# Two attentions: where the lower weight halves stand on DVE, when turned probabilities are copied, and how output pieces are laid between the turnings

## The chip, the cores and the metric

The kernel runs on one core of a Trainium2 chip. The metric is the device time of one execution in microseconds (us), lower is better. Five engines work from queues of their own and meet at semaphores: TensorE (PE, with PEld for its weight loads), DVE (vector), ACT (scalar), GpSimd (POOL) and SP, which only issues transfers here.

## What is computed

Two transformer blocks over 256 tokens of width 1024, in f32, batch 1. What matters here are the two attentions.

```python
# first block: neighbourhood attention (8 heads) beside a windowed one (8 heads, sinks)
proj = h @ w_in[l] + b_in[l]
qa, ka, va, qb, kb, vb, ga, gb = jnp.split(proj, IN_SPLITS, axis=-1)
y_na = neighbourhood_attention(qa, ka, va, na_rpb[l]) @ w_branch_na[l]
y_swa = windowed_gqa_with_sink(qb, kb, vb, swa_sink[l]) @ w_branch_swa[l]
mixed = jax.nn.sigmoid(ga) * y_na + jax.nn.sigmoid(gb) * y_swa
# second block, layer 1: causal window of 128 keys, 16 heads, sinks
q = rope((h @ w_q[j]).reshape(B, S, N_Q_HEADS, HEAD_DIM), cos, sin)
m = swa_sink_attention(q, kk, vv, sinks[j]) @ w_o[j]
```

## The kernel before

All weights are read once, as a stream of units of 128 x 2048 f32 (1 MB). SP loads a unit into one of three buffers `w32` (`load_unit`, L515 and after); ACT writes its upper half `w_hi` (`split`, L675: a copy rounded to the engine's reduced f32), DVE subtracts for its lower half `w_lo` (`split`, L1619). A product is then three matmuls: upper half by the lower part of x, upper by upper, lower by upper (`product`, L1030 to L1032, 256 columns; `wide_product`, L1042 to L1044, 512 columns). A buffer is loaded again once its lower half is made (`w_lo_ready`). `next_split(at, n)` splits the unit three ahead of n.

Every engine's order is written out by hand. Both attentions run in eight periods, p = 0 to 7, of two heads each:

- TensorE: scores of the next pair (`score1`, L1279; `score2`, L1544, with the mask added by a matmul, L1547), then the turning (transpose) of head 2p's probabilities and of head 2p+1's (`turn`, L1290), then both attends (`attend_pair`, L1302). Matmuls of other work stand between them. In the first attention that is one half of a gate unit (`gate_tile`, 24 matmuls) behind each turning. In the second it is the query units U_Q+2 and U_Q+3 (periods 0 and 1, with `partners`, L1507, for the rotation) and then 32 pieces of the output projection. A piece (`out_chunk(q, c, t)`, three wide matmuls) adds chunk c (heads 2c, 2c+1) to half q of the width, for token half t, and the table `out_behind` says which pieces stand ahead of the first turning, behind it, and behind the second.
- DVE: scales the scores and takes the row maxima (`scores_out`, L1733 to L1744; in the second attention `maxima`, L2100 and L2103, straight from PSUM), adds the sinks, later adds up and inverts the sums (`denominators`, L1752, L1754), subtracts for the lower part of the attention output (`attention_out`, L1760), rotates query tiles (`rotate`, L1692 to L1696) and makes lower weight halves.
- ACT: exponentials (`exps`, L730; `exps2`, L979, and the sinks' at L988), the copy of the turned probabilities out of PSUM (`probs_out`, L741), gates or query tiles out of PSUM (L768, `projected` L971), upper weight halves, the upper part of the attention output (`attention_out`, L747).
- GpSimd: multiplies each head's probabilities by the inverted sums, in two instructions (`normalise`, L612). The turning waits for it (`pn_ready`), as the attend waits for ACT's copies (`pt_ready`), and piece (q, c, t) for the lower part of chunk c (`x_ready`, L1760).

The unit U_WO+2 of the output projection is split into the memory of the query input, so ACT may write it only when both query units are through (`slot_free`). Behind the last pieces (chunk 7, four of them) TensorE runs six keep-busy matmuls (L1193) while the norm of the layer is worked out, and the next feed-forward part follows.

## Time and profile before

| | |
|---|---|
| time, median of 3 runs | 875.08 us (874.93 to 875.15) |
| profiled execution, its own time | 875.79 us |
| span of its trace | 874.0 us |
| PE / PEld busy | 851.1 us (97%) / 750.7 us (86%) |
| DVE busy | 643.8 us (74%) |
| ACT busy | 486.1 us (56%) |
| POOL busy | 123.1 us (14%) |
| granted TensorE clock, mean | 1.00 |
| attend of period 2 to attend of period 6, first attention | 101.98 to 139.60 us |
| scores of period 0 to the keep-busy matmuls, second attention | 616.29 to 676.49 us |

The span is what the trace covers, and the execution's own time holds 1.8 us more around it. Matmuls are pipelined: one of 256 columns is shown as 0.28 us long, but the next begins 0.12 us later, so start to start tells what a matmul costs. Idle time in a row is that of its engine just before it, with the instruction that ended it.

### The profile page before, as it was taken

How to read it: one execution, taken by the hardware profiler on the slowest of the kernel's cores; microseconds unless marked ns; L12 is line 12 of the kernel's file. 1: busy time of each engine (PE TensorE's matmuls, PEld its weight loads, DVE VectorE, ACT ScalarE, POOL GpSimd, SP SyncE). 2: the span in 40 equal slices, each digit the busy share in tenths (PEclk: the TensorE clock that was granted, in tenths of full speed). 3: DMA queues.
4: the chain of work that ended last, by engine and by line, in shares of the span. 5: the costliest groups of instructions: out<-in, count | busy, mean ns of one | idle time of the engine just before them, and what ended most of it. 6: DMA issues, size and time to landing. Idle time of an engine off the chain costs nothing.

```text
span 874.0 us, 14394 instructions
## 1 busy us (share of the span) xinstructions
PE 851.1 (97%) x5477; PEld 750.7 (86%) x5477; DVE 643.8 (74%) x848; ACT 486.1 (56%) x711; POOL 123.1 (14%) x132
## 2 busy tenths in 40 slices
PE   8999999999999999989999999999999999999997
PEld 8998988989999999869888888979766888888895
DVE  7777656777855555787888888777856778888876
ACT  5545666445444444465665565574656666655653
POOL 3182120000600000011112001000121121200000
PEclk9999999999999999999999999999999999999999
DMA  8952323646555556533455555425224255555531
GB/s 310 316 222 103 141 101 116 228 187 241 187 208 179 184 187 235 191 145 133 180 193 195 189 192 193 174 115 193 98 97 145 97 175 188 200 189 181 182 136 49
DMA packets 24086, 152.51 MB, mean 175 GB/s; under 512 B 2443, under 2 KB 3683, under 8 KB 7523
## 3 DMA queue, kind: packets, MB, share of 16 engines
q1 hardware_dynamic: 22672, 145.44, 46.7%
q10 hardware_dynamic: 1363, 6.37, 1.9%
q8 instruction: 35, 0.57, 0.3%
q14 instruction: 16, 0.13, 0.1%
HBM read 150.71 MB, written 1.09 MB: 174 GB/s over the span
## 4 chain that ended last, share of the span: by engine, by line
PE 71%; DVE 4%; issue 1%; ACT 1%; POOL 0%; DVEq 0%; POOLq 0%; ACTq 0%
PE ups L1108 14%; PE down L1036 7%; PE ups L1109 7%; PE down L1038 7%; PE down L1037 7%; PE ups L1031 6%; PE ups L1032 6%; PE ups L1030 6%; PE ups L1071 2%; PE ups L1127 1%; PE down L1154 1%; PE down L1156 1%; PE down L1544 1%; DVE w_lo L1619 1%; PE down L1302 1%
## 5 line engine op out<-in xcount | busy, mean ns | idle before, releaser
L1619 DVE TENSOR_TENSOR w_lo<-w,w_hi 128x2048 fp32r<-128x2048 f32 x133 | 318.8, 2402 | 84.8 <-ACT w_hi L675 84.5
L675 ACT ACTIVATE w_hi<-w 128x2048 fp32r<-128x2048 f32 x133 | 254.0, 1912 | 90.6 <-PE down L1038 41.9
L1030 PE MATMUL ups<-x_both,w_hi 128*128 128x256 f32 x736 | 211.3, 287 | 0.0
L1031 PE MATMUL ups<-x_both,w_hi 128*128 128x256 f32 x736 | 208.1, 283 | 0.0
L1032 PE MATMUL ups<-x_both,w_lo 128*128 128x256 f32 x736 | 208.1, 283 | 0.0
L1108 PE MATMUL ups<-x_both,w_hi 128*128 128x512 f32 x512 | 181.3, 398 | 1.3 <-DVE region L2027 1.3
L1109 PE MATMUL ups<-x_both,w_lo 128*128 128x256 f32 x512 | 143.6, 281 | 0.0
L1030 PEld LDWEIGHTS ups<-x_both,w_hi 128*128 128x128 f32 x736 | 141.0, 192 | 1.6 <-issue 0.7
L1031 PEld LDWEIGHTS ups<-x_both,w_hi 128*128 128x128 f32 x736 | 141.1, 192 | 0.7
L1032 PEld LDWEIGHTS ups<-x_both,w_lo 128*128 128x128 f32 x736 | 141.0, 192 | 0.0
L1108 PEld LDWEIGHTS ups<-x_both,w_hi 128*128 128x128 f32 x512 | 96.2, 188 | 25.3 <-DVE w_lo L1619 1.7
L1036 PE MATMUL down<-w_hi,mid 128*128 128x512 f32 x256 | 100.3, 392 | 0.0
L1037 PE MATMUL down<-w_hi,mid 128*128 128x512 f32 x256 | 99.9, 390 | 0.0
L1038 PE MATMUL down<-w_lo,mid 128*128 128x512 f32 x256 | 99.8, 390 | 0.0
L1109 PEld LDWEIGHTS ups<-x_both,w_lo 128*128 128x128 f32 x512 | 96.7, 189 | 0.5
L2035 DVE SCALAR_TENSOR_TENSOR region<-region,par 128x256 f32<-128x256 f32 x176 | 77.3, 480 | 8.8 <-ACT region L927 4.7
L641 POOL TENSOR_TENSOR region<-region 128x512 f32<-128x512 f32 x18 | 34.8, 1932 | 251.8 <-DVE region L2035 251.8
L927 ACT ACTIVATE region<-region,par 128x256 f32<-128x256 f32 x88 | 48.0, 593 | 22.4 <-DVE region L2027 22.2
L604 POOL TENSOR_TENSOR stat<-stat,neg_half 128x1 f32<-128x1 f32 (+1 forms) x17 | 14.6, 859 | 310.1 <-DVE stat L1864 186.9
L1038 PEld LDWEIGHTS down<-w_lo,mid 128*128 128x128 f32 x256 | 48.0, 188 | 10.6
L1036 PEld LDWEIGHTS down<-w_hi,mid 128*128 128x128 f32 x256 | 48.1, 188 | 9.8
L1037 PEld LDWEIGHTS down<-w_hi,mid 128*128 128x128 f32 x256 | 48.2, 188 | 9.0
(228 smaller groups left out, 1090.6 us busy)
## 6 DMA issues: line engine op xcount, KB each, us to landing
w<-w_stream SPq DMA_DIRECT2D x134, 1024.0 KB, 4.8
gates<-vec_store ACTq DMA_DIRECT2D x5, 1024.0 KB, 6.8
region<-rpb SPq DMA_DIRECT2D x2, 768.0 KB, 13.2
gates<-x_in SPq DMA_DIRECT2D x2, 512.0 KB, 3.9
result<-res SPq DMA_DIRECT2D x4, 256.0 KB, 2.0
con<-consts SPq DMA_DIRECT2D x1, 801.0 KB, 8.4
proj<-bands ACTq DMA_DIRECT2D x1, 544.0 KB, 3.5
gates<-vec_store ACTq DMA_DIRECT2D x1, 512.0 KB, 3.7
```

Source lines behind the costliest of these rows:

```text
L675: a.activation(hi_of(n), w32[s][:, :], ACT.Copy).then_inc(w_hi_ready, 1)
L927: ins = a.activation(glu_c[kind][:, t, :], glu_u[kind][:, t, 2:T + 2], ACT.Identity, bias=pdyn(f"conv{layer}", col + 3), scale=pdyn(f"conv ...
L1030: m(out_ap, w_hi[slot][:, w_cols:w_cols + P], xl, start=first, stop=False, skip_group_check=True)
L1031: m(out_ap, w_hi[slot][:, w_cols:w_cols + P], xh, start=False, stop=False, skip_group_check=True)
L1032: return m(out_ap, w_lo[slot][:, w_cols:w_cols + P], xh, start=False, stop=last, skip_group_check=True)
L1036: m(out_ap, xl, w_hi[slot][:, w], start=first, stop=False, skip_group_check=True)
L1037: m(out_ap, xh, w_hi[slot][:, w], start=False, stop=False, skip_group_check=True)
L1038: return m(out_ap, xh, w_lo[slot][:, w], start=False, stop=last, skip_group_check=True)
L1108: m(bank, w_hi[s][:, w], x_both[fill % 2][:, :, c, :], start=(c == 0), stop=False, skip_group_check=True)
L1109: ins = m(bank[:, T:2 * T], w_lo[s][:, w], x_hi[fill % 2][:, c, :], start=False, stop=(c == DC - 1), skip_group_check=True)
L1619: v.tensor_tensor(lo_of(n), w32[s][:, :], hi_of(n).bitcast(F32), ALU.subtract).then_inc(w_lo_ready, 1)
L2035: ins = v.scalar_tensor_tensor(out=glu_c[kind][:, t, :], in0=glu_u[kind][:, t, tap:T + tap], scalar=pdyn(f"conv{layer}", col + tap), in1=g ...
```

## The change

It moves instructions and adds or removes none.

- First attention, DVE: in period p the split of unit U_GATE+p+3 stood last. Now the split of unit U_GATE+p+2 stands behind the scores of the next pair, ahead of their sums; the last one follows period 7.
- Second attention, DVE: the split of U_WO+2 (by `next_split(U_Q + 3)`) goes from period 2 to 3. ACT: the upper half of the same unit from period 1 to 2; the copy of head 2p's turned probabilities goes ahead of both exponentials and the sinks'; a query unit comes out of PSUM behind the second copy.
- Second attention, TensorE: both tiles of U_Q+3 are cut into halves of 12 matmuls, one behind each turning of periods 0 and 1. The pieces go in pairs (both token halves), one pair behind each turning from period 2 on, one more ahead of the first turning of period 3, one behind the last attend.

```diff
--- before.py
+++ after.py
@@ -960,7 +960,7 @@
             fill(FFNPOST0, MIXPRE1, [("kv_g", X_KV), ("mix_pre1", X_Q)])
 
             spans2 = [(0, P), (P, P + T)]
-            ACT_SPLITS = {0: U_Q + 2, 1: U_Q + 3, 4: U_WO, 5: U_WO + 1, 6: U_WO + 2}
+            ACT_SPLITS = {0: U_Q + 2, 2: U_Q + 3, 4: U_WO, 5: U_WO + 1, 6: U_WO + 2}
 
             def sink2(h):
                 return pcol("sink2", h)
@@ -999,15 +999,14 @@
             sinks2(0)
             next_split(STRAIGHT, U_Q + 1)
             for p in range(8):
+                probs_out(16 + 2 * p, P + T)
                 if p + 1 < 8:
                     exps2(2 * p + 2)
-                probs_out(16 + 2 * p, P + T)
-                if p + 1 < 8:
                     exps2(2 * p + 3)
                     sinks2(p + 1)
+                probs_out(16 + 2 * p + 1, P + T)
                 if p < 2:
                     projected(U_Q + 2 + p, 8 + 2 * p)
-                probs_out(16 + 2 * p + 1, P + T)
                 if p in ACT_SPLITS:
                     next_split(STRAIGHT, ACT_SPLITS[p])
                 attention_out(16 + 2 * p + 1, X_O2, p)
@@ -1567,12 +1566,27 @@
                 elif c == DC - 1:
                     ins.then_inc(wo_done, 1)
 
-            out_behind = {1: ((), ((0, 0, 0),), ()), 2: (((0, 0, 1), (0, 1, 0)), ((0, 1, 1),), ()),
...
+            OUT_FIRST = {2: (0, 0), 3: (1, 1), 4: (1, 2), 5: (1, 3), 6: (1, 4), 7: (1, 5)}
+            OUT_SECOND = {2: (0, 1), 3: (0, 2), 4: (0, 3), 5: (0, 4), 6: (0, 5), 7: (0, 6)}
+
+            def out_pair(q, c):
+
+                for t in range(TT):
+                    out_chunk(q, c, t)
+
+            def query_half(t, half):
+
+                n = U_Q + 3
+                s = n % RING
+                if t == 0 and half == 0:
+                    pe.wait_ge(w_lo_ready, n + 1)
+                    pe.wait_ge(up_read, reads_before(n))
+                for c in range(4 * half, 4 * half + 4):
+                    ins = product(up[s][:, t * T:(t + 1) * T], c * UC + t * P, s, x_hi[X_Q % 2][:, c, :],
+                                  x_lo[X_Q % 2][:, c, :], c == 0, c == DC - 1)
+                if t == 1 and half == 1:
+                    ins.then_inc(unit_done, 1)
+
             score2(0)
             tile(STRAIGHT, U_Q + 2, 0, X_Q)
             partners(U_Q + 1, 6)
@@ -1584,21 +1598,24 @@
                     pe.wait_ge(v_ready, 5)
                 if p == 1:
                     partners(U_Q + 2, 8)
-                    tile(STRAIGHT, U_Q + 3, 1, X_Q)
                 if p == 2:
                     partners(U_Q + 3, 10)
-                for piece in out_behind.get(p, ((), (), ()))[0]:
-                    out_chunk(*piece)
+                if p == 3:
+                    out_pair(1, 0)
                 turn(16 + 2 * p, causal_turn)
                 if p == 0:
                     pe.wait_ge(rot_read, 5)
-                    tile(STRAIGHT, U_Q + 3, 0, X_Q)
-                for piece in out_behind.get(p, ((), (), ()))[1]:
-                    out_chunk(*piece)
+                if p < 2:
+                    query_half(p, 0)
+                else:
+                    out_pair(*OUT_FIRST[p])
                 turn(16 + 2 * p + 1, causal_turn)
-                for piece in out_behind.get(p, ((), (), ()))[2]:
-                    out_chunk(*piece)
+                if p < 2:
+                    query_half(p, 1)
+                else:
+                    out_pair(*OUT_SECOND[p])
                 attend2(2 * p)
+            out_pair(1, DC - 2)
             for t in range(TT):
                 for q in range(2):
                     out_chunk(q, DC - 1, t)
@@ -1782,12 +1799,15 @@
                 if p + 1 < 8:
                     scores1(2 * p + 2)
                     scores1(2 * p + 3)
+                if p:
+                    next_split(STRAIGHT, U_GATE + p - 1)
+                if p + 1 < 8:
                     denominators(2 * p + 2, p >= 3)
                 if p:
                     attention_out(X_O1, p - 1)
                 if p + 1 < 8:
                     denominators(2 * p + 3, p >= 3)
-                next_split(STRAIGHT, U_GATE + p)
+            next_split(STRAIGHT, U_GATE + 7)
             attention_out(X_O1, 7)
 
 
@@ -2118,6 +2138,7 @@
                         dve.wait_ge(sink_ready, p + 1)
                     denominators(16 + h, True)
 
+            DVE_SPLITS = {0: U_Q + 1, 1: U_Q + 2, 3: U_Q + 3, 5: U_WO, 6: U_WO + 1, 7: U_WO + 2}
             maxima(0)
             maxima(1)
             sinks2(0)
@@ -2132,10 +2153,8 @@
                     attention_out(X_O2, p - 1)
                 if p < 3:
                     rotate(6 + p, up[(U_Q + 1 + p) % RING], 6 + 2 * p, 2, cos2[:, :], sin2[:, :])
-                if p in (0, 1, 2):
-                    next_split(STRAIGHT, U_Q + 1 + p)
-                if p in (5, 6, 7):
-                    next_split(STRAIGHT, U_WO + p - 5)
+                if p in DVE_SPLITS:
+                    next_split(STRAIGHT, DVE_SPLITS[p])
                 if p + 1 < 8:
                     totals(p + 1)
             attention_out(X_O2, 7)
```

DVE, first attention, from the sums of head 9 (the L1752 and L1754 rows) to the scores of the next pair. In a row the name left of the arrow is what is written; `w_lo` is a lower weight half, `small` the maxima and sums. Before:

```order
L1752 TENSOR_TENSOR small<-small 128x2
L1754 RECIPROCAL small<-small 128x2
L1619 TENSOR_TENSOR w_lo<-w_0,w_hi 128x2048
L1733 SCALAR_TENSOR_TENSOR scores<-down,con 128x512
L1737 TENSOR_REDUCE small<-scores 128x2
L1744 TENSOR_SCALAR small<-small,neg_sink 128x2
L1733 SCALAR_TENSOR_TENSOR scores<-down,con 128x512
L1737 TENSOR_REDUCE small<-scores 128x2
L1744 TENSOR_SCALAR small<-small,neg_sink 128x2
L1752 TENSOR_TENSOR small<-small 128x2
L1754 RECIPROCAL small<-small 128x2
L1760 TENSOR_TENSOR x_both<-ups,x_both 128x256
```

Now (the same place; 17 lines further down in the file):

```order
L1769 TENSOR_TENSOR small<-small 128x2
L1771 RECIPROCAL small<-small 128x2
L1750 SCALAR_TENSOR_TENSOR scores<-down,con 128x512
L1754 TENSOR_REDUCE small<-scores 128x2
L1761 TENSOR_SCALAR small<-small,neg_sink 128x2
L1750 SCALAR_TENSOR_TENSOR scores<-down,con 128x512
L1754 TENSOR_REDUCE small<-scores 128x2
L1761 TENSOR_SCALAR small<-small,neg_sink 128x2
L1636 TENSOR_TENSOR w_lo<-w_0,w_hi 128x2048
L1769 TENSOR_TENSOR small<-small 128x2
L1771 RECIPROCAL small<-small 128x2
L1777 TENSOR_TENSOR x_both<-ups,x_both 128x256
```

The split has changed places with the scaling and maxima of two heads; it now stands between them and their sums.

ACT, second attention, period 0, behind the upper half of U_WO: exponentials (L979), copies (`probs_t`, L741), the query tile (L971), an upper half. Before:

```order
L979 ACTIVATE probs,small<-down,small 128x128
L979 ACTIVATE probs,small<-down,small 128x256
L741 ACTIVATE probs_t<-down 128x384
L979 ACTIVATE probs,small<-down,small 128x128
L979 ACTIVATE probs,small<-down,small 128x256
L988 ACTIVATE small<-small 128x4
L971 ACTIVATE proj<-ups 128x512
L741 ACTIVATE probs_t<-down 128x384
L675 ACTIVATE w_hi<-w_2 128x2048
L747 ACTIVATE x_both<-down 128x256
```

Now:

```order
L741 ACTIVATE probs_t<-down 128x384
L979 ACTIVATE probs,small<-down,small 128x128
L979 ACTIVATE probs,small<-down,small 128x256
L979 ACTIVATE probs,small<-down,small 128x128
L979 ACTIVATE probs,small<-down,small 128x256
L988 ACTIVATE small<-small 128x4
L741 ACTIVATE probs_t<-down 128x384
L971 ACTIVATE proj<-ups 128x512
L675 ACTIVATE w_hi<-w_2 128x2048
L747 ACTIVATE x_both<-down 128x256
```

The copy of head 0 stands ahead of all four exponentials, and the query tile goes behind the copy of head 1.

TensorE, second attention, from the attend of period 6 (heads 12 and 13) into period 7, which has no scores to compute. Before:

```order
L1302 MATMUL down<-probs_t,v_tok 64x256 x2
L1302 MATMUL down<-probs_t,v_tok 64x128 x2
L1042 MATMUL ups<-w_hi,x_both 128x512
L1043 MATMUL ups<-w_hi,x_both 128x512
L1044 MATMUL ups<-w_lo,x_both 128x512
L1042 MATMUL ups<-w_hi,x_both 128x512
L1043 MATMUL ups<-w_hi,x_both 128x512
L1044 MATMUL ups<-w_lo,x_both 128x512
L1290 MATMUL down<-ident,probs 128x128 x3
L1042 MATMUL ups<-x_both 128x512
L1043 MATMUL ups<-x_both 128x512
L1044 MATMUL ups<-x_both 128x512
```

Now:

```order
L1301 MATMUL down<-probs_t,v_tok 64x256 x2
L1301 MATMUL down<-probs_t,v_tok 64x128 x2
L1289 MATMUL down<-ident,probs 128x128 x3
L1041 MATMUL ups<-w_hi,x_both 128x512
L1042 MATMUL ups<-w_hi,x_both 128x512
L1043 MATMUL ups<-w_lo,x_both 128x512
L1041 MATMUL ups<-w_hi,x_both 128x512
L1042 MATMUL ups<-w_hi,x_both 128x512
L1043 MATMUL ups<-w_lo,x_both 128x512
L1289 MATMUL down<-ident,probs 128x128 x3
L1041 MATMUL ups<-x_both 128x512
L1042 MATMUL ups<-x_both 128x512
```

Two pieces (six wide matmuls) stood between the attend and the turning of head 14; now the turning follows at once, and two stand between the turnings.

## Rows read from the trace of the kernel before

**Rows 1.** The page, part 1: busy us, share of the span, instructions.

```profile
PE 851.1 (97%) x5477; PEld 750.7 (86%) x5477; DVE 643.8 (74%) x848; ACT 486.1 (56%) x711; POOL 123.1 (14%) x132
```

**Rows 2.** Waits of PE, 600 to 676 us: total us, times, longest.

```profile
PE ups L1042 <- DVE x_both L1760: 2.8, 4, 1.1
PE down L1302 <- ACT probs_t L741: 2.4, 3, 1.2
```

**Rows 3.** Timeline, PE, first attention: start us, us, engine, line, operation, tiles.

```profile
101.98 0.44 PE L1302 MATMUL down<-probs_t,v_tok 128*64 128x256 f32 x2
...
110.83 0.44 PE L1302 MATMUL ups<-probs_t,v_tok 128*64 128x256 f32 x2
...
139.60 0.44 PE L1302 MATMUL down<-probs_t,v_tok_swa 128*64 128x256 f32 x2 [0.89 <-ACT probs_t L741]
```

**Rows 4.** Timeline, DVE, then ACT, first attention; idle before in brackets.

```profile
122.50 2.29 DVE L1619 TENSOR_TENSOR w_lo<-w,w_hi 128x2048 fp32r<-128x2048 f32 x1 [2.64 <-ACT w_hi L675]
124.70 0.68 DVE L1733 SCALAR_TENSOR_TENSOR scores<-down,con 128x512 f32<-128x512 f32 x1
...
127.86 0.15 DVE L1752 TENSOR_TENSOR small<-small 128x2 f32<-128x2 f32 x1
...
129.17 0.57 ACT L741 ACTIVATE probs_t<-down 128x512 f32<-128x512 f32 x1
```

**Rows 5.** Timeline, PE, second attention, period 5.

```profile
654.15 0.93 PE L1544 MATMUL down<-proj 64*128 64x128 f32 x8
...
655.21 0.53 PE L1042 MATMUL ups<-w_hi,x_both 128*128 128x512 f32 x1
...
656.98 0.47 PE L1042 MATMUL ups<-w_hi,x_both 128*128 128x512 f32 x1
...
658.75 0.48 PE L1042 MATMUL ups<-x_both 128*128 128x512 f32 x1
...
659.63 0.44 PE L1302 MATMUL down<-probs_t,v_tok 128*64 128x256 f32 x2
...
660.43 0.38 PE L1544 MATMUL down<-proj 64*128 64x128 f32 x2
```

**Rows 6.** Timeline, PE, second attention, its start, period 6 and its end.

```profile
615.34 1.02 PE L1507 MATMUL ups<-proj,con 128*128 128x256 f32 x4
616.29 0.93 PE L1544 MATMUL down<-proj 64*128 64x128 f32 x8
...
620.35 0.49 PE L1290 MATMUL down<-ident,probs 128*128 128x128 f32 x3
...
664.01 0.47 PE L1042 MATMUL ups<-x_both 128*128 128x512 f32 x1 [0.52 <-DVE x_both L1760]
...
673.68 0.47 PE L1042 MATMUL ups<-x_both 128*128 128x512 f32 x1 [1.06 <-DVE x_both L1760]
...
676.49 0.50 PE L1193 MATMUL down<-mask_bf,ident_bf 128*128 128x384 bf16 x2
```

**Rows 7.** Timeline, DVE, then POOL, second attention, periods 1 and 5.

```profile
628.78 0.68 DVE L1692 TENSOR_TENSOR gates<-ups,sin 128x512 f32<-128x512 f32 x1
...
657.51 2.28 DVE L1619 TENSOR_TENSOR w_lo<-w,w_hi 128x2048 fp32r<-128x2048 f32 x1
659.71 0.15 DVE L1752 TENSOR_TENSOR small<-small 128x2 f32<-128x2 f32 x1
...
660.15 1.62 POOL L612 TENSOR_SCALAR probs<-probs,small 128x128 f32<-128x128 f32 x4 [5.12 <-DVE small L1754]
```

**Rows 8.** Timeline, ACT, second attention, period 0.

```profile
620.88 0.49 ACT L741 ACTIVATE probs_t<-down 128x384 f32<-128x384 f32 x1 [1.34 <-PE down L1290]
...
622.06 0.21 ACT L988 ACTIVATE small<-small 128x4 f32<-128x4 f32 x1
```

**Rows 9.** Timeline, DVE and POOL, ahead of the first attention's periods.

```profile
75.24 2.27 DVE L1619 TENSOR_TENSOR w_lo<-w,w_hi 128x2048 fp32r<-128x2048 f32 x1
...
75.41 2.89 POOL L612 TENSOR_SCALAR probs<-probs,small 128x256 f32<-128x256 f32 x2 [1.21 <-DVE small L1754]
```

5 rows, old and new, of the table out_behind are left out of this document.

## The prediction

> **What bounds the kernel now.** I read the page first. TensorE is busy for 97% of the span [rows 1], so time can be won only where it waits, and lost only where a new wait begins. Next come the answers on what TensorE waits for in the two stretches that the change touches. In the second attention it waits 2.8 us in 4 places for DVE's lower half of an attention output, and 2.4 us in 3 places for the copied turned probabilities [rows 2]. The reader is to see that neither releaser is a shortage of weights.
>
> Then the timeline, by periods; period p turns and attends heads 2p and 2p+1. In the first attention the attends of periods 2, 3 and 6 begin at 101.98, 110.83 and 139.60 [rows 3]. Period 2 to 3 takes 8.85 us with no wait; the three from 3 to 6 take 28.77, which is 28.77 - 3 x 8.85 = 2.2 us too much, and the last attend names the copy. Why the copy is late stands in DVE's rows: the split sat idle 2.64 us until ACT's upper half came, and only at 124.70, when it was through, could the scores be scaled; ACT's copy at 129.17 comes behind the exponentials of those scores [rows 4]. The next upper half stands behind that copy. Copy, upper half, lower half, scores, exponentials, copy are a closed loop, and it is longer than 8.85 us once the sinks come in (period 3 on).
>
> In the second attention one undisturbed period gives prices [rows 5]: scores 1.06 us (654.15 to 655.21); two pieces and a turning 1.77 (655.21 to 656.98, and 656.98 to 658.75 again), of which I put 1.53 on the pieces and 0.24 on the turning; one piece ahead of an attend 0.88, so a pair 1.6; an attend 0.80. The stretch from the scores of period 0 at 616.29 to the keep-busy matmuls at 676.49 takes 60.2 us [rows 6].
>
> **The change, first attention.** One instruction moves: the lower half of period p's unit leaves the end of DVE's period and stands behind the scores of period p+1. Nothing is added. The loop opens: scores are scaled as soon as TensorE has them, and ACT's upper half is ready a whole period before DVE asks for it. What is late next? DVE's period counts from TensorE's scores: scaling starts about 1.2 in and takes 3.2 for two heads with sinks (124.70 to the sums at 127.86 [rows 4]), the split 2.2, so the sums stand at 6.6 and GpSimd is through with the first head at about 7.9. Its turning is due at 8.85 + 1.06 = 9.9: 2.0 us of cover. The second head has over 4. The transfer into the freed buffer starts some 4 us later, and has two periods, some 17 us, where half of that would do: nothing. **Term: -2.2 us**, bounds 0 (another wait ends at the same place) and -2.4.
>
> **Second attention, the engines.** DVE's row: with the split in a period it begins 3.36 us behind the scores (657.51 - 654.15), the sums 5.56, GpSimd 6.0, 1.62 for two heads, so the first is ready at 6.8 and the second at 7.6 [rows 7]. A rotation adds three instructions like the one at 628.78, together 1.9. ACT's row: copy 0.53 behind its turning (620.35 to 620.88), then 1.18 for the copy and one head's exponentials, until the sinks' at 622.06 [rows 6, 8]. With copies first, two heads' exponentials end at most 0.53 + 2 x 1.18 = 2.9 us behind the first turning. TensorE's row with a wait: the piece that needs the newest output began 3.58 us behind the scores (664.01 - 660.43) [rows 5, 6].
>
> **Period by period.** *0:* up to the first turning nothing moves, 4.06 us [rows 6]; a whole query tile is 4.06 - 1.06 = 3.0, a half 1.5. So 4.06 + 0.24 + 1.5 + 0.24 + 1.6 + 0.8 = 8.4. Exponentials end at 4.06 + 2.9 = 7.0, ahead of DVE's sums (5.56 + 1.9 = 7.5): free. *1:* scores 1.06, partners 0.95 (615.34 to 616.29), then turning, half, turning, half, attend: 6.4. *2:* DVE's sums of period 1 end late, first head ready at 6.8 + 1.9 = 8.7, that is 2.3 in; TensorE is there at 2.0. Turning at 2.4, then 1.77 + 0.24 + 1.6 + 0.8: 6.8. *3:* has three pairs, the first ahead of the turning: 1.06 + 1.77 + 1.77 + 1.6 + 0.8 = 7.0. *4, 5, 6:* scores, turning, pair, turning put TensorE at 1.06 + 0.24 + 1.77 = 3.07, but the second pair needs the output of the period before, ready at 3.58: 0.5 us of waiting that the old order covered with pieces. 3.58 + 1.6 + 0.8 = 6.0 each, 18.0. *7:* no scores now stand ahead, and no pieces either: the turning follows the attend directly. Its head is ready 6.8 behind the scores of a 6.0 us period, so it waits to 0.95. Pair and turning would end at 2.7.
>
> Here a collision comes in that the old order avoids. GpSimd scales the second head until 7.6 - 6.0 = 1.6; DVE's last split starts near 1.0, because ACT's upper half and output copy are done. The one place where these two met shows a price: two scalings, 0.94 us alone, took 2.89 when they began at 75.41 beside a split of 2.27 begun at 75.24 [rows 9]. So the last quarter of the scaling (0.4) runs behind the split: 1.0 + 2.3 + 0.4, turning at 3.8 in place of 2.7. This is a bound from both sides: nothing if GpSimd gets in first, 2.3 at most; I take 1.1, because three of its four instructions should be through. The Trainium skill says it in "SBUF — State Buffer", section "SBUF: two separate sides": the pair of ports shared by DVE and GpSimd is an exclusive lock, and a DVE instruction with two SBUF inputs makes a GpSimd instruction that reads SBUF wait for its whole length. By that rule the cost is there; by the row for period 5 alone, where no split meets a scaling, it is not. The trace agrees with the rule in the place named.
>
> From 3.8: 0.24 + 1.6 + 0.8, then six pieces at 0.70 (twelve matmuls took 676.49 - 673.68 = 2.81, four pieces [rows 6]), 4.2: 10.7. The pair (1, 6) that now stands behind the attend also covers the 1.06 us wait named on the row at 673.68.
>
> Sum: 8.4 + 6.4 + 6.8 + 7.0 + 18.0 + 10.7 = 57.3, against 60.2. **Term: -2.9 us**, -4.0 without the collision. Behind 676.49 the same chain of norm and turnings follows; it hangs on the last four pieces, whose order is the same, so it only shifts. The weights of that stage are asked for about as early as before, except one, 2 to 3 us later with over 10 to spare: nothing.
>
> **Total:** 2.2 + 2.9 = 5.1 us. The durations come from an execution of 875.79 us (span 874.0, 1.8 outside it); the median of the runs shown is 875.08, 0.7 below. I subtract from the median: **870.0 us**.
>
> **Rivals.** A measurement of this kernel can tell about 0.2%, 1.75 us, from no change: faster means under 873.3, slower over 876.8.
>
> *No collision* (22%): GpSimd's last quarter slips in ahead of DVE. For it: the margin is a few tenths. 868.9 us. Own range with the case above: 868.2 to 871.2.
>
> *The second attention gives nothing back* (12%): the waits for scaled probabilities in periods 2 and 7 and for outputs in 4 to 6 are longer than I hold. Against it: each is anchored on a measured offset. 875.1 - 2.2 = 872.9.
>
> *The first gives nothing* (10%): the scaling of the first head, now behind the split, is late by the cover of 2.0 us. 875.1 - 2.9 = 872.2.
>
> *No change* (5%): the waits that go are replaced one by one. For it speaks the 97%. The skill's "Perfetto Trace Analysis", section "Identifying the Most-Contended Engine", says to work on the engine with the highest occupancy, and no matmul goes here; by that rule the time would stay at 875.1. The trace disagrees so far as rows 2 and 3 show waits inside those 97%.
>
> *Slower* (6%): one mechanism, in the second attention. The order now has nothing between the scores and the first turning in periods 4 to 7, so lateness of DVE's sums is paid in full. Should DVE find each upper half missing, and wait X us at the split, the sums, the scaling and the turning come X later; covers are about 1.7 (period 1), 0 (2), 1.2 (4), 1.8 (5), 0.2 (6), 0 (7). With X = 2.3 that is 0.6 + 2.3 + 1.1 + 0.5 + 2.1 + 2.3 = 8.9 and 870.0 + 8.9 = 878.9 us. It decides from X of about 2, where it eats the 5.1 and 1.7 more. Against it: upper halves come out a period ahead, and DVE waits for none in this stretch now.
>
> **How the numbers follow.** My own case has 45%; it, the case without collision and the two halves make 89% faster; same 5%, slower 6%. The range 868.2 to 872.5 holds the first two whole and the case of the second attention alone; it leaves out the dearer side of the fourth, no change and slower, some 20%.
>
> **What would show it.** First attention: attends 8.85 us apart from period 1 to 6, no wait on the copy, DVE's split without idle time for the upper half. Second: attend to attend 6.0 in periods 4 to 6 with 0.5 us waits on DVE's output, a wait of about 0.7 to 1.0 for GpSimd at the first turning of period 7, a scaling of over 2 us there, and 57.3 us in all. I am wrong if the first turning of periods 4 to 6 names GpSimd, or if the attends of the first attention name it.

## The result and the profile after

The changed kernel takes **870.31 us** (median of 4, 868.97 to 870.8), the kernel before 875.12 us beside it (874.93 to 877.15): ratio 0.994, 95% interval 0.9927 to 0.9952. A second measurement, on another occasion, gave 869.98 against 874.95 us, 0.9942 (0.9928 to 0.9955). So it is faster by 4.8 to 5.0 us, where 5.1 had been predicted. The profiled execution took 869.99 us, its span is 868.1 us (before 874.0), at a granted clock of 0.998.

The page of the changed kernel, part 1, in the columns of [rows 1]:

```profile
PE 849.1 (98%) x5477; PEld 750.0 (86%) x5477; DVE 644.1 (74%) x848; ACT 486.3 (56%) x711; POOL 126.1 (15%) x132
```

The counts are those of before: nothing was added. GpSimd is busy 3.0 us longer with the same 132 instructions, a first sign that it is held up somewhere; 2.1 of the 3.0 are found below, in period 7.

**First attention.** The timeline of TensorE in the changed kernel, its attends of periods 2 to 6 (a row holds the eight matmuls of an attend):

```profile
101.46 1.08 PE L1301 MATMUL down<-probs_t,v_tok 128*64 128x256 f32 x8
...
110.30 1.08 PE L1301 MATMUL ups<-probs_t,v_tok 128*64 128x256 f32 x8
...
119.14 1.08 PE L1301 MATMUL down<-probs_t,v_tok_swa 128*64 128x256 f32 x8
...
127.98 1.08 PE L1301 MATMUL ups<-probs_t,v_tok_swa 128*64 128x256 f32 x8
...
136.82 1.08 PE L1301 MATMUL down<-probs_t,v_tok_swa 128*64 128x256 f32 x8
```

They stand 8.84 us apart, all of them, where [rows 3] has 28.77 us for the last three; and none names a copy. What the waits of TensorE between 65 and 150 us hold in the changed kernel is one line, of the work ahead of the periods:

```profile
PE down L1278 <- DVE gates L1709: 1.0, 1, 1.0
```

DVE's timeline shows the opened loop. The lower half starts right behind the second head's scores, with no idle time for ACT's upper half, in place of the 2.64 us of [rows 4]; DVE idles earlier instead, for TensorE's scores, which is what an engine off the path should wait for:

```profile
121.32 0.69 DVE L1750 SCALAR_TENSOR_TENSOR scores<-down,con 128x512 f32<-128x512 f32 x1 [2.34 <-PE down L1278]
...
124.34 0.23 DVE L1761 TENSOR_SCALAR small<-small,neg_sink 128x2 f32<-128x2 f32 x1
124.48 2.28 DVE L1636 TENSOR_TENSOR w_lo<-w,w_hi 128x2048 fp32r<-128x2048 f32 x1
126.68 0.15 DVE L1769 TENSOR_TENSOR small<-small 128x2 f32<-128x2 f32 x1
```

**Second attention.** TensorE's waits between 595 and 672 us (total, times, longest), where [rows 2] has 2.8 and 2.4 us:

```profile
PE down L1289 <- POOL probs L612: 1.9, 2, 1.0
PE ups L1041 <- DVE x_both L1777: 0.6, 3, 0.2
```

The waits on copies are gone, those on DVE's output are shorter and stand at other pieces, and waits for GpSimd are new. Where they stand, the timeline of TensorE shows, first at the start, then from period 6 to the end (in place of [rows 5, 6]):

```profile
613.39 0.93 PE L1543 MATMUL down<-proj 64*128 64x128 f32 x8
...
653.84 0.93 PE L1543 MATMUL down<-proj 64*128 64x128 f32 x8
...
655.03 0.49 PE L1289 MATMUL down<-ident,probs 128*128 128x128 f32 x3
...
656.75 0.49 PE L1289 MATMUL down<-ident,probs 128*128 128x128 f32 x3
657.43 0.47 PE L1041 MATMUL ups<-x_both 128*128 128x512 f32 x1 [0.19 <-DVE x_both L1777]
...
658.96 0.87 PE L1301 MATMUL down<-probs_t,v_tok 128*64 128x256 f32 x8
660.72 0.55 PE L1289 MATMUL down<-ident,probs 128*128 128x128 f32 x3 [0.89 <-POOL probs L612]
...
663.63 0.55 PE L1289 MATMUL down<-ident,probs 128*128 128x128 f32 x3 [0.97 <-POOL probs L612]
...
665.50 0.87 PE L1301 MATMUL down<-probs_t,v_tok 128*64 128x256 f32 x8
...
670.53 1.15 PE L1192 MATMUL down<-mask_bf,ident_bf 128*128 128x384 bf16 x6
```

From the scores of period 0 to keep-busy it is 670.53 - 613.39 = 57.14 us, against 60.2 before. This stretch is the measure of every experiment below; it is called "the stretch". Note the row at 657.43: it names 0.19 us of idle time, but from turning to piece it is 657.43 - 656.75 = 0.68, where an undisturbed turning takes 0.24. The wait is worth 0.44, over twice what the bracket says, because the turning ahead of it has been counted as busy to its end.

The collision, in DVE's and GpSimd's timelines of the changed kernel, period 7 (compare the 1.62 us of [rows 7]):

```profile
660.66 2.30 DVE L1636 TENSOR_TENSOR w_lo<-w,w_hi 128x2048 fp32r<-128x2048 f32 x1
...
659.84 3.73 POOL L612 TENSOR_SCALAR probs<-probs,small 128x128 f32<-128x128 f32 x4 [4.32 <-DVE small L1771]
```

The scaling is through at 659.84 + 3.73 = 663.57, and the second turning begins at 663.63.

### The profile page after: what moved, and what is told of

Same layout as the page of the kernel before. It is cut to its first block, busy times and chain, and to the rows that moved or that the text cites. A ratio compares the mean times of both kernels' runs of the same rounds, so it can differ in the third digit from the quotient of the medians.

```text
span 868.1 us, 14394 instructions
## 1 busy us (share of the span) xinstructions
PE 849.1 (98%) x5477; PEld 750.0 (86%) x5477; DVE 644.1 (74%) x848; ACT 486.3 (56%) x711; POOL 126.1 (15%) x132
## 4 chain that ended last, share of the span: by engine, by line
PE 70%; DVE 5%; issue 1%; POOL 1%; ACT 1%; DVEq 0%; POOLq 0%; ACTq 0%
PE ups L1107 14%; PE down L1035 7%; PE ups L1108 7%; PE down L1037 7%; PE down L1036 7%; PE ups L1030 6%; PE ups L1031 6%; PE ups L1029 6%; PE ups L1070 2%; PE ups L1126 1%; DVE w_lo L1636 1%; PE down L1153 1%; PE down L1155 1%; PE down L1159 1%; PE down L1543 1%
```

## The experiments

Times are medians; each ratio is against the kernel before in the same series, which took 875.12, 875.37 and 874.95 us in the three series (1 to 4, 5 to 8, 9 to 12). The stretch comes from each run's trace, that is from one execution, and compares runs of different series better than the medians do.

| run | us | ratio (95%) | stretch |
|---|---|---|---|
| before | 875.1 | | 60.20 |
| 1 first attention only | 873.43 | 0.9981 (0.9972 to 0.9990) | 60.28 |
| 2 second attention only | 872.02 | 0.9965 (0.9953 to 0.9977) | 57.14 |
| 3 last lower half behind scaling | 868.64 | 0.9926 (0.9913 to 0.9940) | 55.97 |
| 4 output between the maxima | 869.18 | 0.9932 (0.9918 to 0.9945) | 56.33 |
| 5 three mends | 867.91 | 0.9912 (0.9897 to 0.9927) | 54.41 |
| 6 changed, old copies | 869.44 | 0.9933 (0.9919 to 0.9946) | 56.57 |
| 7 before, new copies | 878.11 | 1.0028 (1.0017 to 1.0039) | 62.99 |
| 8 period 7's pieces spread | 868.75 | 0.9923 (0.9909 to 0.9936) | 56.42 |
| 9 last lower half earlier | 871.74 | 0.9963 (0.9949 to 0.9976) | 57.96 |
| 10 before, new pieces | 872.49 | 0.9971 (0.9961 to 0.9982) | 57.38 |
| 11 three mends, old copies | 868.94 | 0.9936 (0.9922 to 0.9950) | 55.94 |
| 12 changed kernel again | 869.98 | 0.9942 (0.9928 to 0.9955) | 57.15 |

**1 and 2: each attention alone.** Run 1 is the kernel before with the one move in the first attention:

```diff
                     scores1(2 * p + 3)
+                if p:
+                    next_split(STRAIGHT, U_GATE + p - 1)
+                if p + 1 < 8:
                     denominators(2 * p + 2, p >= 3)
...
-                next_split(STRAIGHT, U_GATE + p)
+            next_split(STRAIGHT, U_GATE + 7)
```

Run 2 is the changed kernel with that move undone.

> The kernel before with the move in the first attention alone. Theory (the loop through DVE's split is opened, the second attention's gain is separate): attends of the first attention 8.84 us apart in periods 1 to 6, 2.2 us off the time, about 872.9; the second attention keeps its 60.2 us. Rival (most of the gain comes from elsewhere, the start of the run or the second attention): no change that can be told, 874.5 or more.

> The changed kernel with the first attention as it was. Theory: the attends of periods 3 to 6 are 9.2, 9.8 and 9.8 us apart again, the second attention takes 57.1 us instead of 60.2, time about 872.1. Rival (the two gains overlap or depend on each other): under 1.5 us off, or over 4.5.

Run 1 gained 1.7 us and run 2 3.1 us; together 4.8, against 4.8 and 5.0 of the whole. In run 1 the attends stand 8.84 us apart in periods 1 to 6 and the stretch stays at 60.28; in run 2 the attends from period 3 on are 9.17, 9.81 and 9.81 apart again and the stretch is 57.14. The parts don't touch each other.

**3: the collision taken away.** DVE's last lower half of the attention waits until GpSimd is through:

```diff
                 if p in DVE_SPLITS:
+                    if p == 7:
+                        dve.wait_ge(pn_ready, 32)
                     next_split(STRAIGHT, DVE_SPLITS[p])
```

> The changed kernel, where DVE's split in period 7 of the second attention also waits until GpSimd has scaled the last head. Theory (DVE's split holds GpSimd's last instruction off for its whole length): the four scalings take 1.6 us instead of 3.7, the second turning of period 7 waits for nothing, 1.0 us off the changed kernel, about 869.3; the split ends near 1 us later and nobody waits for it. Rival (the scaling is slow for another reason, or the wait only moves to DVE's output or to the last pieces): the scaling still takes over 2.5 us, or the time stays.

868.64 us, a stretch of 55.97. GpSimd's and DVE's timelines of this run:

```profile
659.98 1.62 POOL L612 TENSOR_SCALAR probs<-probs,small 128x128 f32<-128x128 f32 x4 [4.32 <-DVE small L1771]
...
661.63 2.29 DVE L1636 TENSOR_TENSOR w_lo<-w,w_hi 128x2048 fp32r<-128x2048 f32 x1 [0.75 <-POOL probs L612]
```

The same four instructions take 1.62 us instead of 3.73, and the second turning comes at 662.63, 1.77 behind the first and with no wait. The first still waits 0.88 us: that one was never the collision's. A wait of 0.75 us added on DVE shortened the kernel; it gave back 0.2 us, since the norm behind the stretch then waits 0.41 us for DVE in place of 0.20.

**9: the collision made worse.** The same lower half ahead of DVE's output copy of period 7, so that it starts 0.6 us earlier:

```diff
+                if p == 7:
+                    next_split(STRAIGHT, DVE_SPLITS[p])
                 if p:
                     attention_out(X_O2, p - 1)
...
-                if p in DVE_SPLITS:
+                if p in DVE_SPLITS and p < 7:
```

> The changed kernel with DVE's last lower half of the second attention ahead of the output of heads 12 and 13 in place of behind it, so that it starts some 0.6 us earlier, right at the start of GpSimd's last scaling. If the two can't run side by side, one of the four scalings is through and three come behind the 2.28 us of the split: the scaling takes some 3.6 us again, but the first head is ready only some 2.7 us after it begins; the first turning of period 7 comes 1.9 us later than in the changed kernel, the second 0.8 us later, and scores of period 0 to keep-busy take 57.9 us and the kernel 871.1 us. If they run side by side and the 3.7 us have another cause (the output's 256 columns, say): the scaling is through in under 2 us and the time is 869.2 us.

871.74 us, a stretch of 57.96. The median overstates the loss: the profiled execution was the shortest of the five (870.20, where run 12's took 869.82), and the stretch in it is 0.82 us longer than in the changed kernel. The timelines of DVE, GpSimd and TensorE in this run:

```profile
659.36 2.33 DVE L1636 TENSOR_TENSOR w_lo<-w,w_hi 128x2048 fp32r<-128x2048 f32 x1
...
659.19 3.65 POOL L612 TENSOR_SCALAR probs<-probs,small 128x128 f32<-128x128 f32 x4 [4.30 <-DVE small L1771]
...
662.10 0.33 PE L1289 MATMUL down<-ident,probs 128*128 128x128 f32 x1 [2.90 <-POOL probs L612]
```

The length of the scaling is the same as in the changed kernel (3.65 and 3.73), but what waits is another half: now it is the first turning, by 2.90 us, and the second finds its head ready. In both runs the collision costs GpSimd about one length of DVE's instruction; what TensorE pays depends on which of the four scalings is caught.

**4: the output copy between the maxima.** It removes the waits on DVE's output in periods 4 to 6:

```diff
                     maxima(2 * p + 2)
+                if p:
+                    attention_out(X_O2, p - 1)
+                if p + 1 < 8:
                     maxima(2 * p + 3)
                     sinks2(p + 1)
-                if p:
-                    attention_out(X_O2, p - 1)
```

> The changed kernel, where DVE makes the lower part of the attention output between the two heads' maxima instead of behind them and the sinks. Theory (in periods 4 to 6 TensorE waits some 0.45 us each for that output): these waits go, the periods take 5.5 us instead of 5.9, 1.2 to 1.3 us off the changed kernel, about 869.0. Rival (the later maximum makes the second head's exponentials and so the sums late, and the first turnings wait for GpSimd instead): the periods stay at 5.9 us, or period 7 begins with a longer wait.

869.18 us; the stretch is 0.81 shorter (56.33). No wait on DVE's output is left, and periods 4 and 5 take 5.52 us in place of 5.94. Of the 1.3 us for three periods some 0.45 came back: TensorE now reaches period 6 and 7 earlier than GpSimd's heads are ready (turning at 1.37 behind the scores of period 6 in place of 1.19, a wait of 1.07 in period 7 in place of 0.89).

**8: period 7's pieces spread.** One piece ahead of the first turning, two between, one behind:

```diff
+                if p == 7:
+                    out_chunk(1, 5, 0)
                 turn(16 + 2 * p, causal_turn)
...
+                elif p == 7:
+                    out_chunk(1, 5, 1)
+                    out_chunk(0, 6, 0)
                 else:
                     out_pair(*OUT_FIRST[p])
...
+                elif p == 7:
+                    out_chunk(0, 6, 1)
                 else:
                     out_pair(*OUT_SECOND[p])
```

> The changed kernel with period 7's four pieces one ahead of the first turning, two between the turnings, one behind. The collision stays: the second turning still comes when GpSimd is through with its last quarter, at the same time as in the changed kernel. If so the wait ahead of the first turning shrinks from 0.9 to 0.2 us, the wait ahead of the second grows or stays near 1, and one piece fewer (0.70 us) stands behind it: 869.6 us. If the first turning itself comes later by the piece and starts ACT's copy later: no gain, 870.3.

868.75 us; the stretch is 56.42, 0.72 shorter: one piece. The first turning stands where it stood (1.75 behind the attend, 1.76 in the changed kernel), with the piece inside the wait, and the second still waits 0.97 us for GpSimd, since the collision is untouched.

**6, 7, 10 and 11: which part of the second attention earns it.** Run 6 is the changed kernel with ACT's first copy behind the next head's exponentials, as before:

```diff
             for p in range(8):
-                probs_out(16 + 2 * p, P + T)
                 if p + 1 < 8:
                     exps2(2 * p + 2)
+                probs_out(16 + 2 * p, P + T)
+                if p + 1 < 8:
                     exps2(2 * p + 3)
```

Run 7 is the kernel before with ACT's new order of copies and nothing else. Run 10 is the kernel before with TensorE's new order of the second attention and nothing else. Run 11 is run 5 (below) with the diff of run 6.

> The changed kernel with ACT's old order: each first copy behind the exponentials of the next head, which need that head's maxima. Theory A: the new place of the copies earns nothing once the pieces are spread, because a pair of pieces (1.5 us) between the turnings covers a copy that comes 0.9 us later, and in periods 4 to 6 a later second turning runs into time that waits for DVE's output anyway: 870.3 to 870.8 us, at most 0.2 us more a period, no wait over 0.3 us on a copy. Theory B, the copies are what gives the 2.4 us (the waits on copies in the kernel before): they come back, 872.0 to 872.7.

> The kernel before with the new place of ACT's copies alone (pieces, halves of query tiles and lower halves as before). Theory A (pieces and copies are two mends of the same waits): the 2.4 us of waits on copies in the second attention go, the 2.8 us on DVE's output stay: 60.2 us from the scores of period 0 to keep-busy become some 58, and 872.7 to 873.5 us. Theory B, the copies help only with the new order of pieces: 874.5 to 875.1. In both the first attention keeps its 2.2 us of waits.

> The kernel before with TensorE's new order in the second attention alone: the first attention, the places of the lower and upper halves and ACT's order of copies are the old ones. If the pieces earn it all, the stretch from the scores of period 0 to keep-busy takes what the changed kernel with the old order of copies took, 56.6 us where the kernel before took 60.2: 871.5 us. If the new places of the two halves of one unit (period 2 to 3 on DVE, 1 to 2 on ACT) are needed, the rotation and the split now stand together in period 2 and period 3's first turning waits for GpSimd, by at most the 1.9 us of a rotation less 0.6 of cover: up to 1.3 us more, 872.8 us.

> The version with the three mends together, with ACT's old order of copies (first copy behind the exponentials of the next head). With the waits on DVE's output gone, a second turning that waits 0.5 us for the copy is paid in full: 0.5 to 0.7 us in each of periods 4, 5 and 6, nothing given back in period 7, since DVE's last split there waits for GpSimd by order. 867.9 + 1.7 = 869.6 us. The rival: the copies' new place earns nothing here either (as in the changed kernel, where the old order was 0.6 us shorter over the stretch): 867.3 to 868.0 us.

Run 6 came out a little *shorter* than the changed kernel: 869.44 us and a stretch of 56.57, 0.57 less. Theory B is out, but theory A said at best "the same" and saw no wait over 0.3 us. The waits are there; TensorE's, between 595 and 680 us in run 6:

```profile
PE down L1290 <- ACT probs_t L741: 1.6, 3, 0.5
PE down L1290 <- POOL probs L612: 0.6, 1, 0.6
```

Each of periods 4 to 6 takes 6.23 us instead of 5.93, 0.9 together: I was wrong that the output's wait would swallow the later second turning whole. But period 7 gives 1.5 back. Of that 1.1 lies between its turnings (1.77 us in place of 2.91), because the collision is gone, and 0.3 ahead of the first, which waits less for its head behind a longer period 6. GpSimd and DVE in run 6:

```profile
661.11 1.63 POOL L612 TENSOR_SCALAR probs<-probs,small 128x128 f32<-128x128 f32 x4 [4.61 <-DVE small L1772]
...
662.29 2.60 DVE L1637 TENSOR_TENSOR w_lo<-w,w_hi 128x2048 fp32r<-128x2048 f32 x1
```

The lower half is ready to start 1.18 us behind the scaling in place of 0.82, because ACT's output copy, on which DVE's depends, ran later. Asked for that late, it doesn't hold GpSimd up at all, and it is DVE's instruction that takes 0.32 us longer. So 0.4 us in DVE's start changed who waits, and the side effect is larger than the effect. (Run 10 shows the same pair again: scaling 1.63 us, lower half begun 1.18 us in, 2.59 us.)

Run 11 asks the same with the collision ruled out by order: there the old copies cost 1.53 us in the stretch (55.94 against 54.41). The medians, from two series, put it at 1.0 us as they stand and at 2.1 by the ratios. The new place of the copies is right; in the changed kernel it is paid for by the collision that it brings about.

Run 7 fell out of both theories: 878.11 us, 2.7 us slower than the kernel before, a stretch of 62.99. Its waits, and then a turning and an attend in TensorE's and ACT's timelines:

```profile
PE down L1301 <- ACT probs_t L741: 4.8, 7, 1.5
PE ups L1041 <- DVE x_both L1759: 2.8, 4, 1.1
```

```profile
652.18 0.49 PE L1289 MATMUL down<-ident,probs 128*128 128x128 f32 x3
653.34 0.52 PE L1289 MATMUL down<-ident,probs 128*128 128x128 f32 x3
655.33 0.87 PE L1301 MATMUL down<-probs_t,v_tok 128*64 128x256 f32 x8 [0.78 <-ACT probs_t L741]
...
652.71 0.49 ACT L741 ACTIVATE probs_t<-down 128x384 f32<-128x384 f32 x1 [3.27 <-PE down L1289]
...
654.77 0.51 ACT L741 ACTIVATE probs_t<-down 128x384 f32<-128x384 f32 x1
```

ACT stands idle 3.27 us in front of the first copy while exponentials that could run wait behind it; then two heads' exponentials stand between the two copies (652.71 to 654.77, 2.1 us), and TensorE, which has one piece of work between its second turning and the attend, waits for the second copy. Waits on copies double, from 2.4 to 4.8 us. The first copy's new place, worth 1.5 us of the stretch to run 5, costs the kernel before some 2.5 us: its sign hangs on the surrounding order, here on how much of TensorE's work lies between its second turning and the attend. (Run 7 also moves the query output, but only in periods 0 and 1. These two take 0.3 us more than in the kernel before, periods 2 to 7 together 2.5.)

Run 10, TensorE's order alone, has 872.49 us and a stretch of 57.38: 2.8 of the 3.1 us of the whole change. My alternative for it (period 3 waits for GpSimd) is wrong: no turning of period 3 waits, so the new places of the two weight halves earned nothing that shows here, where period 1 ends later. What it lacks is in period 1 (7.60 us in place of 6.47), where ACT's query output stands ahead of the second copy and itself waits for TensorE's query half, behind the second turning. TensorE's timeline of run 10:

```profile
628.13 0.49 PE L1290 MATMUL down<-ident,probs 128*128 128x128 f32 x3
...
631.12 0.87 PE L1302 MATMUL down<-probs_t,v_tok 128*64 128x256 f32 x8 [1.07 <-ACT probs_t L741]
```

ACT's query output behind the second copy, a part of the change to which the prediction gave no price of its own, is worth this 1.1 us in its period; run 6, which has the new place, does not have the wait. Period 2 gives 0.3 of it back (6.39 us in place of 6.73), since its first turning no longer waits for GpSimd, and the whole stretch is 0.8 us longer than run 6's.

**5: the three mends together,** that is the diffs of runs 3, 4 and 8.

> The changed kernel with three mends of the second attention together: DVE's last lower half behind GpSimd's last scaling, DVE's output between the maxima of the two heads, and in period 7 one piece ahead of the first turning, two between the turnings, one behind. If the three act in different places: the scaling again 1.6 us in place of 3.7 and the second turning of period 7 without its wait (-1.2 us, as measured alone), the three 0.4 us waits on the output gone (-0.8, as measured alone), and a piece of 0.70 us in the wait of some 0.9 ahead of period 7's first turning (-0.7): scores of period 0 to keep-busy 54.4 us where the changed kernel took 57.1, and 867.5 us. The rival, that period 7 hangs on ACT's and GpSimd's chain and the piece only moves the wait elsewhere: 868.2 or more.

**867.91 us**, 0.9912 of the kernel before: 7.5 us faster than it, and 2.1 to 2.4 faster than the changed kernel (2.7 by the stretch). The stretch is 668.12 - 613.71 = 54.41 us, as worked out (54.4). What is left of waits between 595 and 680 us in this run:

```profile
PE down L1202 <- DVE res L2001: 0.6, 2, 0.4
PE down L1289 <- POOL probs L612: 0.2, 1, 0.2
```

This version beats both kernels.

**12: the changed kernel again,** unedited.

> The changed kernel as it is, beside the others on one chip: 870.3 us by its first measurement, span of the stretch 57.1 us. The versions measured one by one lay 0.3 to 0.6 us lower against it than their traces say; if that was the changed kernel's first measurement, this one gives some 869.9.

869.98 us and a stretch of 57.15. From keep-busy to the end of the span it is 197.5 to 198.0 us in the kernel before and in every run: behind the stretch everything only shifts. What differs between executions otherwise lies ahead of it: in the nine profiled runs that have the new first attention and the new pieces, the stretch begins between 612.75 and 614.04 us, 1.3 us that no edit here explains. That is why the medians follow the stretches only to within some 0.6 us, and run 9's to 0.9.

## Why the prediction was right

*First attention, -2.2 us.* From the first attend to the eighth it took 63.09 us before and 60.84 after: -2.25. The loop was the cause, since run 1, which changes the one instruction's place, brings every distance of periods 1 to 6 to 8.84. The cover of 2.0 us for the first head was right too: in period 5 DVE's sums (the row at 126.68) begin 6.5 us behind the scores (120.15), GpSimd is through with the head at 128.06, 7.9 behind them, and the turning begins 2.0 later, at 130.06.

*Second attention, by periods,* predicted and measured: 8.4 and 8.48; 6.4 and 6.47; 6.8 and 6.73; 7.0 and 6.90; 18.0 and 17.79 for periods 4 to 6; 10.7 and 10.77. Sum 57.3 and 57.14. The errors are 0.1 us or less each but for periods 4 to 6 together. There the second pair began 3.59 us behind the scores, where 3.58 had been put: the 0.2 us come from the pair ahead of the attend, 1.53 us and not 1.6, and from rounding 5.98 up to 6.0. The wait for GpSimd at period 2's first turning was there too: the partners' matmuls and what follows them take 1.15 us in place of 0.86, and the turning stands 2.34 behind the scores where 2.4 was put. No releaser is named there, but GpSimd's scaling of the period begins at 629.80, its first half is done 0.8 later, and the turning begins at 630.68.

*Period 7.* The first turning was put at 0.95 and came at 0.96 us (from 659.76, where the attend of period 6 ends), the second at 3.8 and came at 3.87. Without the collision it was put at 2.7; run 3 shows 2.73. So 1.1 us had been taken from bounds of 0 and 2.3, and 1.14 was right, but partly by luck and not for the stated reason. I held that three of the four scalings would be through when DVE starts. The trace shows that two were. GpSimd's timeline in the changed kernel, the third and the fourth scaling of period 7 by themselves:

```profile
660.64 2.48 POOL L612 TENSOR_SCALAR probs<-probs,small 128x128 f32<-128x128 f32 x1
...
663.10 0.47 POOL L612 TENSOR_SCALAR probs<-probs,small 128x256 f32<-128x256 f32 x1
```

The third takes 2.48 us in place of 0.37, and the fourth runs behind it. The prediction's own figures say as much: at 1.62 / 4 = 0.4 us each, two are through when DVE starts 1.0 us behind the first. It came to nearly the same because DVE started 0.1 us earlier than put (at 0.90 in the period, not 1.0) and held GpSimd for 2.2 us, not 2.3, while the second scaling that was caught added only its own 0.4. Run 9 reads alike: begun 0.17 us in, one is through, the second ends at 662.04, and the first turning begins at 662.10.

*The rule on the ports.* GpSimd's scaling took 3.73 and 3.65 us when a lower half began inside it and 1.62 when none did, from the same operands; and 2.60 instead of 2.28 fell on DVE when GpSimd was in first. The Trainium skill's "SBUF — State Buffer", section "SBUF: two separate sides", has this as an exclusive lock that goes to whichever of the two instructions starts first. The trace agrees that either side can be the one that waits; which one started first the rows can't tell (last section). Runs 3 and 9 show that this meeting sets TensorE's wait ahead of the turning whose head it catches.

*The rivals.* "No collision" (868.9 us) is what run 3 is: 868.64. "The second gives nothing" fell by run 2 and "the first gives nothing" by run 1. "No change", for which the 97% of TensorE spoke, fell too: the Trainium skill's "Perfetto Trace Analysis", section "Identifying the Most-Contended Engine", says to optimise the engine with the highest occupancy first, but for TensorE it judges the headroom by the matmul work done and by the share of weight loads (86% here), not by matmul busy time. So it does not say that the time stays, as the prediction read it. TensorE was the one that gained, through the order of its own work and of that of DVE and ACT. "Slower" did not come: no lower half in periods 1 to 6 waits for its upper half, and no first turning of periods 4 to 6 names GpSimd. That a slower kernel lies nearby is shown by run 7, by a mechanism that the prediction did not have among its rivals. One slip is in how the chances follow: the range also leaves out the case at 872.9 (12%), so with no change and slower it leaves out at least 23%, not some 20%.

*Two things that the prediction missed.* It put no price on ACT's query output moving behind the second copy (1.1 us in period 1, run 10), and it did not see that the first copy's new place, with the rest of the change, lost 0.57 us (run 6) through the collision. The sum was right because it was made on the final order as a whole, period by period; a sum of gains edit by edit would have been wrong: the stretch is 2.8 us longer for ACT's new order alone, 2.8 shorter for the pieces alone, and 3.1 shorter for all of it. The two stages together are 5.3 us shorter in the traces and 4.8 to 5.0 in the medians, where 5.1 was put; the difference lies within what executions differ by ahead of the stretch.

*Left open.* Lower and upper halves of U_WO+2 in their old places were run only with ACT's old order (run 10); whether they cost something with the new one wasn't tried. Nor was it tried what decides which of GpSimd and DVE waits.

## What to carry to other kernels

In a kernel of queues worked in order, price the final order by periods from offsets ("so long behind the scores"), not the edits one by one: an instruction put earlier in a queue holds up all behind it until its own input is there, so the same move can win 1.5 us in one surrounding and lose 2.5 in another. Where TensorE waits for GpSimd, look first at whether a long DVE instruction lies in the same window, and order the two explicitly: a wait of 0.75 us on DVE bought 1.2 us. An engine at 97% of the span could still be made 7.5 us faster without taking work from it.

## What was unexpected of the hardware

Who loses a meeting of DVE and GpSimd changed within some 0.4 us: with the lower half begun 0.82 us into a scaling of 1.62, GpSimd lost 2.1 us; at 1.18 us in (runs 6 and 10), GpSimd lost nothing and DVE 0.3. The start times in the rows don't tell who will: in the changed kernel the third scaling is shown to begin at 660.64, 0.02 us ahead of the lower half, and it lost; in run 6 the fourth is shown to begin at 662.26, 0.03 us ahead, and DVE lost. And when GpSimd loses, it loses about the same (3.65 us when DVE began 0.17 us in, 3.73 when 0.82 us in).
